# Residual additions ahead of the next evacuation, a row factor made in the feed-forward loop, last output units in halves, first feed-forward tile in two banks

## The chip, the cores and the metric

The kernel runs on one core of a Trainium2 chip. That core has a matrix engine (TensorE, PE in the profile), three engines for elementwise work (VectorE or DVE, ScalarE or ACT, GpSimd or POOL) and a queue engine (SP) that starts most transfers. Each engine runs its own list of instructions in order, and they meet at semaphores. The metric is the device time of one execution in microseconds (us), less is better. Before the change three runs gave 1392.92, 1395.47 and 1396.48 us; the median is 1395.47.

## The reference, cut to what matters

Two blocks of two layers each work on 256 tokens of width 1024, all in float32. The first block has a differential attention layer and a latent attention layer, each followed by a gated feed-forward with a convolution of width 3 and by an embedding that is gated by the residual stream:

```
for i in range(DEPTH):                       # DEPTH = 2
    hn = rms_norm(h, attn_norm[i])
    ...                                      # diff_attention or mla_attention gives mix
    h = h + mix
    h = h + conv_gated_ffn(rms_norm(h, ffn_norm[i]), ffn_w_in[i], ffn_conv_w[i], ffn_conv_b[i], ffn_w_out[i])
    h = h + per_layer_embedding(h, p[i], ple_norm[i], ple_w_proj[i], ple_w_gate[i])

def per_layer_embedding(h, p_i, norm_g, w_proj, w_gate):
    gate = jax.nn.sigmoid(rms_norm(h, norm_g) @ w_gate)
    return (p_i @ w_proj) * gate
```

The second block has a stream x of 256 tokens and a context of 256 tokens. Vectors computed from a conditioning input scale, shift and gate them:

```
mod_x = (silu_c @ w_mod[i] + b_mod[i])[:, None, :]
...
sh_x, sc_x, g_x = jnp.split(mod_x, 3, axis=-1)
hx = rms_norm_2(x, norm_g[i]) * (1.0 + sc_x) + sh_x
hc = rms_norm_2(ctx, norm_g[i]) * (1.0 + sc_c) + sh_c
...                                          # layer 0: grouped attention, layer 1: neighbourhood attention
x = x + g_x * yx
if not last:
    ctx = ctx + g_c * yc
```

## The kernel before, in words

Everything is kept feature-major: `H` holds the residual stream as 8 chunks of 128 features by 256 tokens, `CX` the context. Each product of float32 numbers is made of three matrix products with operands split in a high and a low part (`mm3`, lines 410 to 412). The high part of the activations is in `XH`, the low one in `XL`; of the weights in `WH` and `WL`.

**Weights.** SP reads 295 panels of 128x1024 into six raw slots, in a fixed order (`STREAM`). ScalarE copies a panel to `WH` (line 1729, 1.06 us), VectorE subtracts to `WL` (line 1079, 1.2 us or more). There are only three such pairs of slots (`SPL`), so a panel is split when the third one before it has been used by TensorE. Both engines issue these splits at written places between their other work: a call `ahead(p)` issues all that are due up to panel p+2. What an engine does between two such calls delays the panel that comes next.

**Outputs.** Most products run in units: 128x512 of output in one of two banks, `G0` and `G1` in turn; a unit of a plain product is 2 columns of tiles, 8 input chunks and 3 matmuls, so 48 matmuls of 256 columns, on two panels. A wide unit is 24 matmuls of 512 columns (256 of x and 256 of the context) on one panel. VectorE or ScalarE evacuates a unit and frees its bank. Four more banks are called `A`, and `R` and `O` are two more.

**Norms.** The sum of squares over features is a product with a matrix of ones (`row_stats`, line 464; `col_stats`, line 482, when the result is wanted per token). Squares are made on GpSimd (`squares`, 4 instructions of 128x512, or `sum_of_squares`, which also adds them up, 7 instructions, so that one part instead of four goes through TensorE). ScalarE takes the root (line 1739), VectorE the reciprocal (line 1094). In the first block this factor is applied to the outputs, so products may start before it is there. In the second block it is applied to the inputs: `modulated` has VectorE write x times scale times factor to `XT` (line 1494), ScalarE add the shift and write `XH` (line 2028), and VectorE write `XL` (line 1499), chunk by chunk.

**The places that the change touches**, in the order in which they run, for both layers of the first block where not said otherwise:

- `ffn`: the input projection has 22 tiles of two columns. Tile 0 (`hidden(0, ...)`) needs chunks 6 and 7 of the input last, because they come from the last unit of the attention's output product. All 24 matmuls of its first column come before the 24 of the second. Then come `row_stats`, tile 1, and a loop of tiles with the output projection, which adds up in the four `A` banks.
- `ple`: the small projection `pp` (4 units of 12 matmuls in `G0` and `G1`), then 16 matmuls that turn gathered modulator rows to columns (`turn_gathered`, line 566), then the gate product `pg` (4 units of 48 matmuls). For each unit u of `pg`, VectorE evacuates with the factor (line 1114), ScalarE applies the sigmoid (line 2015), GpSimd multiplies with the projection (line 2354), VectorE adds to `H` (line 1480). In layer 0 the inputs of the next layer (`x_high` and `x_rest` of attn1) are made in between; in layer 1 the context's input for the second block (factor `ac` and `modulated(0, 1, CX, ...)`).
- `l1_dq`: the first product of latent attention, 8 chunks of 6 matmuls of 512 columns; then `col_stats("l1", ...)` with four parts.
- `context_ahead` (layer 1 of the first block is over): 6 chunks of the context go through the query weights while the stream's factor `a` is made; then `row_stats("a")` with four parts, and `wide_unit(0, ...)`, which needs the stream's inputs.
- `a_o`: 8 wide units give the output of the second block's attention; then `row_stats("b")` and the units of `b_q`, whose inputs need `H` after all eight.

## Time and profile before

| what | value |
|---|---|
| median of three runs | 1395.47 us |
| profiled execution, device time | 1392.69 us |
| its span, first to last instruction | 1391.0 us |
| mean granted TensorE clock | 0.979 |
| PE busy | 1297.7 us (93%), 8860 matmuls |
| DVE busy | 948.9 us (68%) |
| ACT busy | 716.7 us (52%) |
| POOL busy | 402.4 us (29%) |
| HBM read | 189.41 MB, 137 GB/s |

The span and the time of the same execution differ by 1.7 us, which lie before the first and behind the last instruction. Busy shares are of the span. A matmul in the trace is shown with its full latency, and the next begins before it ends, so the pace of a row of matmuls is read from their starts, or from a count in a stretch. A row of the timeline reads: start, length, engine, line, operation, output<-inputs, shapes, count; in brackets the idle time of the engine ahead of it and what ended that.

### The profile page before, as it was taken

How to read it: one execution, taken by the hardware profiler on the slowest of the kernel's cores; microseconds unless marked ns; L12 is line 12 of the kernel's file. 1: busy time of each engine (PE TensorE's matmuls, PEld its weight loads, DVE VectorE, ACT ScalarE, POOL GpSimd, SP SyncE). 2: the span in 40 equal slices, each digit the busy share in tenths (PEclk: the TensorE clock that was granted, in tenths of full speed). 3: DMA queues.
4: the chain of work that ended last, by engine and by line, in shares of the span. 5: the costliest groups of instructions: out<-in, count | busy, mean ns of one | idle time of the engine just before them, and what ended most of it. 6: DMA issues, size and time to landing. Idle time of an engine off the chain costs nothing.

```text
span 1391.0 us, 24271 instructions
## 1 busy us (share of the span) xinstructions
PE 1297.7 (93%) x8860; PEld 1122.2 (81%) x8860; DVE 948.9 (68%) x1427; ACT 716.7 (52%) x1244; POOL 402.4 (29%) x390
## 2 busy tenths in 40 slices
PE   6999989999997999998999999699989997999996
PEld 5887979999986876897999998588845586987656
DVE  6868677888866896656888886745257546553674
ACT  5555445555665676544565565433357513412662
POOL 4942234445422140143444542203002311000012
PEclk9999999999998999999999999999999998999999
DMA  8574346666633542153666663222300082532100
GB/s 303 174 233 147 108 140 204 229 222 214 213 117 105 171 133 80 67 191 116 218 226 216 223 211 108 90 92 76 105 16 1 22 210 68 188 104 91 46 1 31
DMA packets 52665, 191.72 MB, mean 138 GB/s; under 512 B 6048, under 2 KB 6304, under 8 KB 52320
## 3 DMA queue, kind: packets, MB, share of 16 engines
q1 hardware_dynamic: 43488, 158.59, 34.3%
q0 software_dynamic: 8368, 31.33, 7.1%
q8 instruction: 62, 1.02, 0.3%
q10 hardware_dynamic: 720, 0.57, 0.1%
q14 instruction: 27, 0.22, 0.1%
HBM read 189.41 MB, written 1.05 MB: 137 GB/s over the span
## 4 chain that ended last, share of the span: by engine, by line
PE 74%; DVE 8%; ACT 7%; issue 7%; POOL 2%; DMA 1%; SPq 0%; DVEq 0%; ACTq 0%; POOLq 0%
PE G L410 13%; PE G L412 12%; PE G L411 12%; PE A L410 6%; PE A L411 5%; PE A L412 5%; PE R L631 3%; DVE WL L1079 2%; ACT WH L1729 2%; PE R L557 2%; PE R L537 2%; PE R L410 1%; PE R L412 1%; PE R L411 1%; PE A L963 1%
## 5 line engine op out<-in xcount | busy, mean ns | idle before, releaser
L1079 DVE TENSOR_TENSOR WL<-RAW,WH 128x1024 fp32r<-128x1024 f32 x295 | 395.1, 1345 | 296.0 <-ACT WH L1729 295.4
L1729 ACT ACTIVATE WH<-RAW 128x1024 fp32r<-128x1024 f32 x295 | 310.3, 1057 | 407.3 <-PE G L412 287.9
L410 PE MATMUL G<-XH,WH 128*128 128x256 f32 (+1 forms) x1368 | 414.5, 303 | 25.4 <-DVE WL L1079 9.5
L411 PE MATMUL G<-XL,WH 128*128 128x256 f32 (+1 forms) x1368 | 410.9, 300 | 0.0
L412 PE MATMUL G<-XH,WL 128*128 128x256 f32 (+1 forms) x1368 | 410.5, 300 | 0.0
L410 PEld LDWEIGHTS G<-XH,WH 128*128 128x128 f32 x1368 | 265.7, 194 | 39.8 <-issue 16.6
L411 PEld LDWEIGHTS G<-XL,WH 128*128 128x128 f32 x1368 | 266.1, 194 | 8.4
L412 PEld LDWEIGHTS G<-XH,WL 128*128 128x128 f32 x1368 | 266.0, 194 | 7.3
L410 PE MATMUL A<-HH,WH 128*128 128x256 f32 x352 | 99.7, 283 | 0.9 <-POOL HL L2333 0.9
L411 PE MATMUL A<-HL,WH 128*128 128x256 f32 x352 | 99.6, 283 | 0.0
L412 PE MATMUL A<-HH,WL 128*128 128x256 f32 x352 | 99.5, 283 | 0.0
L2309 POOL CAST XH<-HRS 128x256 fp32r<-128x256 f32 x24 | 11.4, 474 | 282.7 <-DVE HRS L1653 282.7
L1160 DVE TENSOR_REDUCE SM<-A 128x2 f32<-128x1024 f32 (+1 forms) x80 | 67.9, 850 | 15.2 <-PE A L963 13.5
L410 PE MATMUL G<-WH,XH 128*128 128x512 f32 x136 | 56.4, 415 | 17.3 <-DVE XL L1105 11.2
L410 PEld LDWEIGHTS A<-HH,WH 128*128 128x128 f32 x352 | 67.5, 192 | 2.2 <-ACT WH L1729 1.9
L410 PE MATMUL A<-WH,XH 128*128 128x512 f32 (+1 forms) x144 | 58.1, 403 | 11.5 <-DVE XL L1499 6.1
L411 PEld LDWEIGHTS A<-HL,WH 128*128 128x128 f32 x352 | 67.5, 192 | 0.1
L412 PEld LDWEIGHTS A<-HH,WL 128*128 128x128 f32 x352 | 67.6, 192 | 0.0
L1768 ACT ACTIVATE ATT<-R 128x1024 f32<-128x1024 f32 (+3 forms) x56 | 37.7, 673 | 57.1 <-PE R L631 57.1
L2329 POOL TENSOR_TENSOR HRS<-ATT,HRS 128x256 f32<-128x256 f32 x22 | 31.8, 1444 | 120.1 <-ACT HRS L1934 120.1
L2329 POOL TENSOR_TENSOR HRS<-HSQ,HRS 128x256 f32<-128x256 f32 x22 | 31.8, 1444 | 102.2 <-ACT HRS L1934 102.2
L411 PE MATMUL A<-WL,XH 128*128 128x512 f32 (+1 forms) x144 | 56.4, 391 | 0.0
(346 smaller groups left out, 2474.7 us busy)
## 6 DMA issues: line engine op xcount, KB each, us to landing
RAW<-in_wst SPq DMA_DIRECT2D x295, 512.0 KB, 3.8
M<-in_wmod POOLq DMA_DIRECT2D x48, 512.0 KB, 4.1
B<-in_rpb POOLq DMA_DIRECT2D x4, 1024.0 KB, 11.9
H<-in_x_t SPq DMA_DIRECT2D x2, 512.0 KB, 8.4
M<-in_x_tok SPq DMA_DIRECT2D x1, 1024.0 KB, 13.3
M<-in_ctx_t POOLq DMA_DIRECT2D x1, 1024.0 KB, 6.6
out_y<-M SPq DMA_DIRECT2D x2, 384.0 KB, 2.7
C<-in_cst SPq DMA_DIRECT2D x1, 737.0 KB, 15.4
```

The source lines that it names most:

```text
L410: mm(out, lh, rh, start=start, stop=False, skip_group_check=True)
L411: mm(out, lh, rl, start=False, stop=False, skip_group_check=True)
L412: return mm(out, ll, rh, start=False, stop=stop, skip_group_check=True)
L537: m = mm(out[32 * g:32 * g + 32, q * P:(q + 1) * P], SC[:, k, :], RM[:, i % RMS, k * P:(k + 1) * P], start=(k == 0), stop=(k == KD - 1), s ...
L557: m = mm(O[0:32, :], SCR[:, 2 * s + c, :], w[:, 512 * c:512 * c + 512], start=(s == 0 and c == 0 and w is RH), stop=(s == 3 and c == 1 and ...
L631: m = nc.tensor.transpose(ST[c][:, k * P:(k + 1) * P], PRB[a % 3][:, c, k * P:(k + 1) * P], IDT)
L963: m = mm(out[c][:, 0:nk * P], Q2[64 * c:64 * c + 64, t, qt * P:(qt + 1) * P], K2[64 * c:64 * c + 64, t // 4, k0:512], start=True, stop=Tru ...
L1079: v.tensor_tensor(WL[:, slot, :], RAW[:, raw, :], WH[:, slot, :].bitcast(F32), ALU.subtract).then_inc(w_lo, 1)
L1160: v.tensor_reduce(small(80, a, 2), sc, AX, ALU.max, negate=True).then_inc(at_mx, 1)
L1729: act(WH[:, slot, :], RAW[:, raw, :], ACT.Copy).then_inc(w_hi, 1)
L1768: act(att(s, j)[:, 0:width, 0:nk, q * P:(q + 1) * P], RO[:, :].rearrange("p (l k q) -> p l k q", l=2, k=4)[:, 0:width, 0:nk, :], ACT.Copy) ...
L2329: g.tensor_tensor(HID[b], CB[b][:, 0, :], SG[b], ALU.mult).then_inc(f_hid, 1)
```

## The change

- `ffn`, tile 0: its second column goes to bank `A[3]`; chunks 0 to 5 of both columns come first, then 6 and 7 of both. VectorE evacuates it in two instructions.
- `ple`: units 2 and 3 of `pp` go to `A[0]` and `A[1]`. The 16 turning matmuls become transposes of 32 rows, and VectorE adds the pieces with one reduction. In the loop over the units of `pg`, the addition of unit u-1 and the inputs made from it stand ahead of the evacuation of unit u, on VectorE and on ScalarE.
- The factor `ac` and the first of the three steps of `modulated` for the context move from `ple(1)` into `ffn(1)`; the other two steps stay in `ple(1)`.
- The sums of squares `l1` and `a` are added up on GpSimd, so one part goes through TensorE for each. `row_stats("a")` stands after five chunks of `context_ahead` instead of after all six.
- `a_o`: units 5, 6 and 7 are made in halves: first x of all three (24 matmuls of 256 columns each, banks `A[1]` to `A[3]`), then the context of all three. The sums for `b` and the first inputs for `b_q` go in between.

The core of the diff (the helper functions that split `modulated` in two are the old code cut in two):

```diff
-                hidden(0, p0, u0 % 2, u0 // 2, p0, XS[tag])
+                pe.wait_ge(bank_free[u0 % 2], u0 // 2)
+                for ks in (range(6), range(6, KD)):
+                    for c in range(2):
+                        take(p0 + c)
+                        for k in ks:
+                            x_come(XS[tag], k, KD)
+                            wh, wl = wtile((p0 + c) % SPL, k)
+                            m = mm3((A[3] if c else G[u0 % 2])[:, 0:T], wh, wl, XH[:, k, :], XL[:, k, :], k == 0, k == KD - 1)
+                        if k == KD - 1:
+                            m.then_inc(w_used, 1)
...
                 for u in range(4):
-                    gemm_unit(U0[a] + u, START[a] + u // 2, 4 * (u % 2), 2, 8, 2)
+                    if u >= 2:
+                        pe.wait_ge(h_upd, 8 * layer + u - 1)
+                    gemm_unit(U0[a] + u, START[a] + u // 2, 4 * (u % 2), 2, 8, 2, out=A[u - 2] if u >= 2 else None)
...
-                    m = mm(O[:, 2 * t:2 * t + 2], YR[0:4, 512 + t * P:512 + (t + 1) * P], SEL, start=True, stop=True,
-                           skip_group_check=True)
+                    m = nc.tensor.transpose(O[:, 32 * t:32 * t + 32], YR[:, 512 + t * P:512 + (t + 1) * P], IDT[0:32, 0:32])
...
+                def added(u):
+
+                    dv.wait_ge(p_m, 4 * layer + u + 1)
+                    v.tensor_tensor(flat2(H, u), flat2(H, u), PG[:, u % 2, :], ALU.add).then_inc(h_upd, 1)
+
+                for u in range(4):
+                    e = START[b] + 2 * u + 2
+                    ahead(e - 1)
+                    if u == 0:
+                        row_factor(b, 0)
+                    else:
+                        added(u - 1)
+                        if layer == 0:
+                            x_rest(H, "attn1", 0, 2 * u, 2 * u - 2)
+                        elif u < 3:
+                            modulated_rest(0, 1, range(4 * u - 4, 4 * u))
+                    if u >= 2:
+                        dv.wait_ge(h_upd, 8 * layer + 4 + u - 1)
+                    evac(U0[b] + u, e, PG[:, u % 2, :].rearrange("p (a t) -> p a t", a=2), 0)
+                    ahead(e)
+                added(3)
...
+            for u in range(5, 8):
+                part_o(u, A[u - 4][:, 0:T], 0).then_inc(ao_x, 1)
+                if u == 6:
+                    row_stats("b", R, range(0, 2))
+            for u in range(5, 8):
+                part_o(u, bank(U0["a_o"] + u)[:, T:512], 8).then_inc(w_used, 1)
+                if u == 5:
+                    row_stats("b", R, range(2, 4))
...
-            squares("l1", H, updated(4))
+            sum_of_squares("l1", H, updated(4))
...
-            squares("a", H, updated(12))
+            sum_of_squares("a", H, updated(12))
```

VectorE in `ple(0)`, from the factor to the evacuation of the last unit of `pg`. `ATP<-G,RST` is an evacuation, `H<-H,ATP` an addition, `XL<-H,V,XH` an input of the next layer. Before:

```order
L1094 RECIPROCAL RST<-RST 128x256 [waits row_rt]
L1114 TENSOR_TENSOR ATP<-G,RST 128x512 [waits w_used,row_ok]
L1079 TENSOR_TENSOR WL<-RAW,WH 128x1024 [waits w_hi] x2
L1114 TENSOR_TENSOR ATP<-G,RST 128x512 [waits w_used]
L1480 TENSOR_TENSOR H<-H,ATP 128x512 [waits p_m]
L1079 TENSOR_TENSOR WL<-RAW,WH 128x1024 [waits w_hi] x2
L1114 TENSOR_TENSOR ATP<-G,RST 128x512 [waits w_used,h_upd]
L1480 TENSOR_TENSOR H<-H,ATP 128x512 [waits p_m]
L1079 TENSOR_TENSOR WL<-RAW,WH 128x1024 [waits w_hi]
L1105 SCALAR_TENSOR_TENSOR XL<-H,V,XH 128x256 [waits x_hi] x2
L1079 TENSOR_TENSOR WL<-RAW,WH 128x1024 [waits w_hi]
L1114 TENSOR_TENSOR ATP<-G,RST 128x512 [waits w_used,h_upd]
```

The same stretch of VectorE now, where the names are the same and the lines are those of the changed kernel:

```order
L1121 RECIPROCAL RST<-RST 128x256 [waits row_rt]
L1141 TENSOR_TENSOR ATP<-G,RST 128x512 [waits w_used,row_ok]
L1106 TENSOR_TENSOR WL<-RAW,WH 128x1024 [waits w_hi] x2
L1527 TENSOR_TENSOR H<-H,ATP 128x512 [waits p_m]
L1132 SCALAR_TENSOR_TENSOR XL<-H,V,XH 128x256 [waits x_hi] x2
L1141 TENSOR_TENSOR ATP<-G,RST 128x512 [waits w_used]
L1106 TENSOR_TENSOR WL<-RAW,WH 128x1024 [waits w_hi] x2
L1527 TENSOR_TENSOR H<-H,ATP 128x512 [waits p_m]
L1132 SCALAR_TENSOR_TENSOR XL<-H,V,XH 128x256 [waits x_hi] x2
L1141 TENSOR_TENSOR ATP<-G,RST 128x512 [waits w_used,h_upd]
```

Each addition and its two input instructions moved from behind the next evacuation to ahead of it.

VectorE at the end of `a_o` and the start of `b_q`. `H<-G,MD,H` adds the x part of a unit, `M<-G,MD,M` its context part (`CX` lies in `M`); `M<-H,GS,RST` and `XL<-M,MD,XH` make the inputs. Before, from the x part of the last unit:

```order
L1661 SCALAR_TENSOR_TENSOR H<-G,MD,H 128x256 [waits w_used]
L1663 SCALAR_TENSOR_TENSOR M<-G,MD,M 128x256
L1094 RECIPROCAL RST<-RST 128x256 [waits row_rt]
L1494 SCALAR_TENSOR_TENSOR M<-H,GS,RST 128x256 [waits row_ok]
L1494 SCALAR_TENSOR_TENSOR M<-H,GS,RST 128x256 x7
L1499 SCALAR_TENSOR_TENSOR XL<-M,MD,XH 128x256 [waits x_hi] x8
```

The same place now, from the x parts of the last three units:

```order
L1702 SCALAR_TENSOR_TENSOR H<-A,MD,H 128x256 [waits ao_x] x3
L1707 SCALAR_TENSOR_TENSOR M<-G,MD,M 128x256 [waits w_used]
L1106 TENSOR_TENSOR WL<-RAW,WH 128x1024 [waits w_hi]
L1121 RECIPROCAL RST<-RST 128x256 [waits row_rt]
L1434 SCALAR_TENSOR_TENSOR M<-H,GS,RST 128x256 [waits row_ok]
L1434 SCALAR_TENSOR_TENSOR M<-H,GS,RST 128x256 x3
L1707 SCALAR_TENSOR_TENSOR M<-G,MD,M 128x256 [waits w_used]
L1442 SCALAR_TENSOR_TENSOR XL<-M,MD,XH 128x256 [waits x_hi] x4
L1106 TENSOR_TENSOR WL<-RAW,WH 128x1024 [waits w_hi]
L1434 SCALAR_TENSOR_TENSOR M<-H,GS,RST 128x256 x4
L1442 SCALAR_TENSOR_TENSOR XL<-M,MD,XH 128x256 [waits x_hi] x4
```

The context parts and two weight splits now stand among the steps that make the inputs of `b_q`, and these come four chunks at a time.

## Rows read from the trace of the kernel before

**Rows 1.** Page, part 4, the chain that ended last by engine

```profile
PE 74%; DVE 8%; ACT 7%; issue 7%; POOL 2%; DMA 1%; SPq 0%; DVEq 0%; ACTq 0%; POOLq 0%
```

**Rows 2.** Waits of PE: engine line <- releaser: total us, times, longest

```profile
PE G L410 <- DVE XL L1105: 17.6, 5, 11.2
PE G L410 <- DVE WL L1079: 9.5, 7, 2.2
```

**Rows 3.** Windows, PE alone: stretch, its length, busy (x matmuls), clock, DMA share, GB/s

```profile
1112.00:1132.00 20.00, 20.00 (x90) 1.00 1.01 241
1182.00:1202.00 20.00, 20.00 (x169) 1.00 0.59 198
1156.00:1166.00 10.00, 4.51 (x21) 0.50 0.01 2
...
852.00:856.00 4.00, 4.00 (x23) 0.57 0.40 137
```

**Rows 4.** Timeline, PE, tile 0 of the feed-forward in layers 0 and 1

```profile
177.10 0.36 PE L410 MATMUL G<-XH,WH 128*128 128x256 f32 x1 [2.19 <-DVE XL L1105]
...
181.81 1.02 PE L464 MATMUL R<-RSQ,C 128*128 128x256 f32 x4
...
628.91 0.35 PE L410 MATMUL G<-XH,WH 128*128 128x256 f32 x1 [2.60 <-DVE XL L1105]
...
635.12 1.02 PE L464 MATMUL R<-RSQ,C 128*128 128x256 f32 x4
```

**Rows 5.** Timeline, PE, ple of layer 0 and the start of l1_dq

```profile
391.71 0.39 PE L410 MATMUL G<-XH,WH 128*128 128x256 f32 x1 [0.93 <-ACT B L1986]
...
394.78 3.77 PE L566 MATMUL R<-C,B 4*128 4x2 f32 x32
...
406.43 0.47 PE L410 MATMUL G<-XH,WH 128*128 128x256 f32 x1
...
425.71 0.47 PE L410 MATMUL G<-WH,XH 128*128 128x512 f32 x1 [0.90 <-issue]
```

**Rows 6.** Timeline, ACT, after the evacuation of unit 1 of pg

```profile
414.69 0.63 ACT L2015 ACTIVATE ATP<-ATP 128x512 f32<-128x512 f32 x1 [2.32 <-DVE ATP L1114]
415.23 2.10 ACT L1729 ACTIVATE WH<-RAW 128x1024 fp32r<-128x1024 f32 x2
```

**Rows 7.** Timeline, DVE, the same unit and the last of layer 1

```profile
416.30 2.61 DVE L1079 TENSOR_TENSOR WL<-RAW,WH 128x1024 fp32r<-128x1024 f32 x2 [1.05 <-ACT WH L1729]
...
419.76 0.68 DVE L1480 TENSOR_TENSOR H<-H,ATP 128x512 f32<-128x512 f32 x1
...
422.89 0.87 DVE L1105 SCALAR_TENSOR_TENSOR XL<-H,V,XH 128x256 fp32r<-128x256 f32 x2
...
885.23 0.68 DVE L1114 TENSOR_TENSOR ATP<-G,RST 128x512 f32<-128x512 f32 x1
```

**Rows 8.** Timeline, PE, chunk 6 of l1_dq, col_stats and the next product

```profile
438.13 0.47 PE L410 MATMUL G<-WH,XH 128*128 128x512 f32 x1 [2.39 <-issue]
...
442.39 1.99 PE L482 MATMUL R<-C,RSQ 128*128 128x2 f32 x16
...
449.85 0.61 PE L410 MATMUL A<-WH,XH 128*128 128x320 f32 x1 [2.70 <-ACT WH L1729]
```

**Rows 9.** Groups by line, POOL: busy us, mean ns of one, idle before

```profile
L2251 POOL TENSOR_TENSOR RSQ<-H 128x512 f32<-128x512 f32 x10 | 13.9, 1404 | 20.8 <-PE R L482 12.8 <-DVE H L1712 8.1
...
L2269 POOL TENSOR_TENSOR RSQ<-RSQ 128x512 f32<-128x512 f32 x4 | 6.9, 1730 | 0.3
```

**Rows 10.** Timeline, PE, from the context's product to wide_unit

```profile
877.39 0.35 PE L410 MATMUL G<-XH,WH 128*128 128x256 f32 x1 [2.14 <-DVE WL L1079]
...
893.72 1.89 PE L464 MATMUL R<-HSQ,C 128*128 128x256 f32 x8
...
901.74 0.77 PE L410 MATMUL A<-WH,XH 128*128 128x512 f32 x1 [6.13 <-DVE XL L1499]
```

**Rows 11.** Timeline, PE, from the sums for b to the end of unit 0 of b_q

```profile
1152.87 1.13 PE L464 MATMUL R<-ATP,C 128*128 128x256 f32 x4 [1.39 <-POOL ATP L2251]
...
1161.49 0.55 PE L410 MATMUL G<-XH,WH 128*128 128x256 f32 x1 [7.49 <-DVE XL L1499]
...
1169.44 1.89 PE L464 MATMUL R<-HSQ,C 128*128 128x256 f32 x8
```

**Rows 12.** Groups by line, DVE

```profile
L1094 DVE RECIPROCAL RST<-RST 128x256 f32<-128x256 f32 x9 | 15.8, 1750 | 14.6 <-ACT RST L1739 14.6
...
L1494 DVE SCALAR_TENSOR_TENSOR M<-H,GS,RST 128x256 f32<-128x256 f32 x16 | 7.9, 561 | 0.1
```

More of the change, by code:

```diff
@@ L429, in x_come, with gemm_unit @@
                     pe.wait_ge(x_lo, fresh - per * (kt - 1 - k))
-            def gemm_unit(u, p, first, kt, x, ncol, width=T, xh=XH, xl=XL, fresh=None, per=1):
-                out = bank(u)
+            def gemm_unit(u, p, first, kt, x, ncol, width=T, xh=XH, xl=XL, fresh=None, per=1, out=None):
+                if out is None:
+                    out = bank(u)
                 i = first
@@ L854, in _ @@
                     token_unit(u, 0, 512, 2, XS["l1"] - KD)
-                    col_stats("l1", R, [RSQ[:, i % 2, :] for i in range(4)])
+                    col_stats("l1", R, [RSQ[:, 0, :]])
                 elif name == "ckv":
@@ L1452, in ffn @@
                     turn(j % 2, (u0 + j) % 2, j, p, p + 3, p + 3, hb + j)
+                    if layer == 1 and j == 2:
+                        row_factor("ac", 1)
+                    elif layer == 1 and j < 5:
+                        modulated_full(0, 1, CX, range(4 * j - 12, 4 * j - 8))
                 with dv.Fori(0, GROUPS) as i:
@@ L1919, in ffn @@
                 root(tag, 0, D)
+                if layer == 1:
+                    root("ac", 1, D, R[:, T:2 * T])
                 ahead(p0 + 2)
@@ L2184, in _ @@
             attention("a")
-            for u in range(8):
+            for u in range(6):
                 ahead(START["a_o"] + u + 1)
             root("b", 0, D)
-            modulated(1, 0, 16, range(KD))
+            modulated(1, 0, 16, range(4))
+            ahead(START["a_o"] + 7)
+            modulated(1, 0, 16, range(4, KD))
             for u in range(4):
```

127 lines of the change are left out of this document (68 added, 59 removed).

## The prediction, made before the changed kernel was run

> **What bounds the kernel now.** I first read the chain that ended last. TensorE holds 74% of it, VectorE and ScalarE 8% and 7%, transfers 1% [rows 1]. So a change pays where it removes matmul time or a hole between matmuls, and a faster transfer pays nothing. Next I read TensorE's waits. The largest sums are for the low part of the inputs and for the low part of the weights [rows 2]. 11.2 us of the first lie at the very start, which the change leaves alone. The timeline of TensorE at the places that the change names then shows holes of 2.19 and 2.60 us in tile 0 of the feed-forward [rows 4], 0.93 us in pp [rows 5], 2.70 us behind the sums of l1 [rows 8], 2.14 and 6.13 us ahead of the second block [rows 10], and 1.39 and 7.49 us between a_o and b_q [rows 11].
>
> I read two paces of matmul from the windows. 90 of 512 columns in 20 us make 0.222 us each, and 169 of 256 columns in 20 us make 0.118 us each, both at a clock of 1.00 [rows 3], which is the 2.4 GHz level. So halving a matmul's width nearly halves its time. The clock is part of the account too. After the turning matmuls it is 0.57 for 4 us. Around the hole of 7.49 us it is 0.50, the 1.2 GHz level, from 1156 to 1166 [rows 3]. A unit of 48 matmuls that costs 48 x 0.118 = 5.7 us elsewhere took 1169.44 - 1161.49 = 8.0 us there [rows 11]. A filled hole can therefore give back about 1.5 to 2.3 us of slow matmuls besides itself.
>
> The sum is made against the profiled execution, 1392.69 us for a span of 1391.0, so it is in microseconds of that trace. The median of the three runs is 2.8 us higher, and I take the difference off the median.
>
> **Tile 0 of the feed-forward, gain 4.0.** The last two chunks of input arrive as late as before. Of the 24 matmuls of the second column, 18 now run ahead of them, so the sums start 18 x 0.118 = 2.1 us earlier than 181.81 [rows 4]. What follows is a chain through the root, the reciprocal, the evacuation and the next split, and it keeps its length. The evacuation in two pieces adds an estimated 0.2 us to it, since a DVE instruction of half the width costs a little more than half. Layer 0 gives 1.9. In layer 1 the first wait to the sums took 635.12 - 628.91 = 6.2 us, against 181.81 - 177.10 = 4.7 us in layer 0 [rows 4]. The 1.5 us more are the slow clock, and a hole cut from 2.60 to about 0.4 us should spare them. Against that stand the root of ac on ScalarE in front of the next split (about 0.4 us), and a reciprocal of 1.75 us and 8 products of 0.56 us [rows 12] that VectorE now does among tiles 2 to 4. Its idle time per tile there is about as long as each insertion, so only the first, straight behind a wait, should be felt: 0.9 us. Layer 1 gives 2.1 + 1.5 - 0.2 - 0.4 - 0.9 = 2.1. Bounds of the pair: 2 (clock slow anyway, all insertions felt) to 5.7.
>
> **Front of ple, 3.8 us earlier in each layer.** The hole of 0.93 goes, since units 2 and 3 of pp wait for no bank. The 16 turning matmuls are 32 records and took 3.77 us, 0.118 each [rows 5], as long as a matmul of 256 columns. The trace shows no transpose of this shape. From above each takes what the pair takes (gain 0). From below it costs one record (gain 1.9). I take 1.9, since a record of 4x2 already costs the least that TensorE shows here. With 1 us of the slow clock behind them this puts the start of unit 1 of pg at 402.6 instead of 406.43 [rows 5]. At that point the panel behind it limits, not TensorE.
>
> The clock at 852 to 856 is 0.57 right behind matmuls that touch 4 rows and 2 columns [rows 3]. Transposes of 32 rows might keep the clock up or might not. The Trainium skill ("TensorE: Matmul & The Clock Gate", Part 4: PE-mode transpose) says that transposes do not count as activity of TensorE for the clock. That speaks against this part of the change. By it the slow stretch stays and unit 1 starts 1.1 us later in each layer, 2.2 us in all, which would make the forecast 1378. No run here shows it yet.
>
> **The moved additions, a loss of 5.3 inside ple(0).** Evacuation u+1 now stands behind the addition of unit u and behind the inputs made from it. From one evacuation to the next VectorE and ScalarE then need: evacuation 0.68, sigmoid 0.63, two copies of a panel 2.10 [rows 6], the second subtraction 1.3 of the 2.61, addition 0.68 [rows 7], ScalarE's high parts about 0.9, and half of the 0.87 for the low parts [rows 7]. Together that is 6.8 us. TensorE needs 5.7 for a unit. So ple(0) is no longer paced by TensorE but by this ring: the first evacuation at 405.6 (402.6, plus the split of the next panel 1.3 and the reciprocal 1.75 [rows 12]), the fourth at 405.6 + 3 x 6.9 = 426.3 (0.1 for the semaphores), and l1_dq starts at 427.2 instead of 425.71 [rows 5]. The 3.8 us of the front are spent, and 1.5 more.
>
> **l1_dq and its sums, net gain of layer 0 5.5.** The inputs of chunks 0 to 5 are now ready when l1_dq starts. The fourth weight panel still is not. ScalarE copies it behind ten input copies in both kernels, so chunk 6 starts at 437.6, about where it did (438.13 [rows 8]), and the product ends at 440.4. Before it ended at 442.39 [rows 8]. The sums then have a quarter of the matmuls: 1.2 us instead of 449.85 - 2.70 - 442.39 = 4.8 [rows 8]. The wait of 2.70 behind them stays, because ScalarE still issues the next panel only behind the root. The next product starts at 440.4 + 1.2 + 2.7 = 444.3 instead of 449.85 [rows 8]: 5.5 us. What hides the longer work of GpSimd is l1_dq itself. Seven instructions, 4 x 1.40 + 3 x 1.73 = 10.8 us [rows 9], begin behind the fourth evacuation, sigmoid and product, at 429.2, and end at 440.0, 0.4 us before they are wanted. If that cover goes, each us shows. Bounds: 2.5 to 7.
>
> **Layer 1, from pp to the first product with x, gain 3.0.** The front gives 3.8 as in layer 0. The hole of 2.14 [rows 10] came from context work between the evacuations. It shrinks to about 1.5, since the copy for that panel now waits behind the later evacuation of unit 1. The last evacuation stood at 885.23, well behind TensorE [rows 7], and comes at about 879, so GpSimd begins its squares 6.3 us earlier. But it has 10.8 us of work instead of 4 x 1.40 = 5.6 [rows 9], 5.2 us more. TensorE has done five of six chunks by then and waits for the sum. The sums go from eight matmul pairs to two, about 2.8 us less of TensorE, but most of these ran beside the squares, so I count 1.9. The factor is ready 6.3 - 5.2 + 1.9 = 3.0 us earlier, and the hole of 6.13 behind it [rows 10] becomes 4.7 plus the sixth chunk: 901.74 becomes 898.7. Bounds: 0.5 to 5.5.
>
> VectorE works beside those GpSimd instructions, and these additions took 1.73 us in the mean against 1.40 of the squares [rows 9]. The Trainium skill ("SBUF — State Buffer", Who interferes with whom) says that a VectorE instruction with two SBUF inputs and a GpSimd instruction that reads SBUF exclude each other for whole instructions. By it the seven instructions keep these means or go above them, towards the first rival below.
>
> **a_o in halves, gain 7.0.** Three units of 24 wide matmuls become 48 narrow ones each: 3 x (48 x 0.118 - 24 x 0.222) = 1.0 us added. From the last sums at 1152.87 to b_q at 1161.49 lie 8.6 us of root, reciprocal and inputs [rows 11]. Now two context halves, 48 x 0.118 = 5.7 us, run beside them, and only 4 of the 8 first steps stand ahead of chunk 0 (4 x 0.56 = 2.2 us [rows 12]). So chunk 0 waits for nothing, and chunk 4 waits about 2.6 us for the second four and the weight split between them. Holes of 1.39 + 7.49 = 8.9 become 2.9: 6.0 less. The slow clock cost unit 0 of b_q 8.0 - 5.7 = 2.3, of which I count 2.0. Sum: 6.0 + 2.0 - 1.0 = 7.0. Bounds: 4.5 (a new slow stretch) to 8.
>
> **Sum.** 4.0 + 5.5 + 3.0 + 7.0 = 19.5 us. The median goes from 1395.5 to 1376.0.
>
> **Rivals.**
> - *The ring and the sums on GpSimd take ple and what follows back.* If the ring is 8 us instead of 6.8, and GpSimd needs 2 us per instruction, the 5.5 and 3.0 go to zero: 19.5 - 8.5 = 11 us, 1384.5. For it: both have almost no slack (0.4 us in l1_dq). Against it: the long rows of GpSimd stand beside heavy VectorE work, which is thinner after the last evacuation.
> - *The clock gives more.* If the slow stretches in l1_dq, behind the sums of l1 and ahead of the second block all go too, at 1.5 to 2 us each, and tile 0 gives its upper bound, the gain is about 27: 1368.5. Against it: these stretches stand behind holes that remain in part.
> - *Slower.* The moved addition couples the units fully: the copy of unit u+2's first panel waits for the evacuation of unit u+1. Then TensorE (5.7) and the way from an evacuation to a ready panel (0.68 + 0.63 + 1.05 + 1.3 = 3.6) run one after the other in all 8 units: 8 x 3.6 = 29 us on top of the forecast, 1405. It decides once an evacuation ends later than the unit behind it begins its second half. Against it: the first panel of unit u+2 is issued right behind the sigmoid of unit u, with a unit of 5.7 us to spare.
> - *No change.* The waits move to the weight splits everywhere, and the gain stays below 4 us.
>
> **How the numbers follow.** Forecast 0.58, the ring and GpSimd 0.22, more from the clock 0.10, no change 0.05, slower 0.05. The range goes from 1368 to 1387, which takes in the first two rivals and the bounds (gains of 9 to 27). A measurement of this kernel can tell about 0.3%, 4 us, from no change. Faster by more than that: 0.58 + 0.22 + 0.10 = 0.90, taken as 0.89; within it 0.06; slower 0.05.
>
> **What would show it.** Right: between the first wait of tile 0 and its sums about 2.5 us in both layers; no wait in pp; 16 transposes in under 2 us; four evacuations of ple(0) 6.8 us apart; sums of l1 in 1.2 us; unit 0 of b_q with a wait near 2.6 us and a clock of 1.00. Wrong: evacuations at TensorE's pace of 5.8 us (the gain in layer 0 grows), a wait of TensorE for GpSimd ahead of the sums of l1, a clock of 0.5 behind the transposes or in b_q, or new waits of more than 1 us in tiles 3 to 5 of ffn(1).

## The result

| kernel | median | runs | ratio to the kernel before, 95% interval |
|---|---|---|---|
| before | 1395.08 us | 4 (1392.92 to 1396.48) | |
| changed | 1380.97 us | 4 (1380.17 to 1383.41) | 0.9903 (0.9885 to 0.9922) |

The change makes the kernel 14.1 us faster, by the medians. The prediction was 1376.0 with a range of 1368 to 1387. So the sign and the range were right, and the forecast was 5.0 us too low. Two later executions, 3170.83 us of "order undone" and 4345.82 of "GpSimd waits", stand apart from all others and are left out below.

The profiled execution of the changed kernel took 1383.41 us for a span of 1381.7. It was the slowest of its four, while that of before (1392.69) was quicker than the four runs in the table. So the two traces differ by 9.3 us only. TensorE's mean granted clock was 0.976 in it and 0.979 before. (1 - clock) x span is the time that TensorE's clock withheld: 33.2 us against 29.2. So the clock withheld 4.0 us more in this trace than in that of before; without that the two would differ by an estimated 13.3 us, near the 14.1 of the medians.

The chain of the changed kernel by engine, to be held against [rows 1]:

```profile
PE 72%; DVE 10%; ACT 8%; issue 5%; POOL 2%; DMA 1%; SPq 0%; DVEq 0%; ACTq 0%; POOLq 0%
```

VectorE has gained 2 points of it. TensorE's waits in the changed kernel (total, times, longest) show where, against [rows 2]:

```profile
PE R L466 <- POOL RSQ L2340: 7.0, 1, 7.0
...
PE G L411 <- DVE ATP L1141: 4.7, 1, 4.7
PE G L411 <- issue: 4.2, 1, 4.2
```

They are 7.0 us for GpSimd's sum, 4.7 for an evacuation, and 4.2 put down to "issue". The first two are new; the third stood at the same chunk before, with 2.39 us [rows 8]. The next rows, the timeline of TensorE in the changed kernel, say where they lie:

```profile
178.97 1.02 PE L466 MATMUL R<-RSQ,C 128*128 128x256 f32 x4
...
199.26 0.36 PE L411 MATMUL G<-XH,WH 128*128 128x256 f32 x1 [2.37 <-DVE WL L1106]
...
392.27 1.19 PE L568 MATMUL R<-C,B 32*128 32x32 f32 x16
394.50 0.55 PE L411 MATMUL G<-XH,WH 128*128 128x256 f32 x1 [1.04 <-ACT B L2057]
401.77 1.02 PE L466 MATMUL R<-RSQ,C 128*128 128x256 f32 x4
...
426.69 0.76 PE L411 MATMUL G<-WH,XH 128*128 128x512 f32 x1 [4.69 <-DVE ATP L1141]
441.78 0.47 PE L411 MATMUL G<-WH,XH 128*128 128x512 f32 x1 [4.22 <-issue]
446.20 0.95 PE L484 MATMUL R<-C,RSQ 128*128 128x2 f32 x8
449.85 0.60 PE L411 MATMUL A<-WH,XH 128*128 128x320 f32 x1 [2.70 <-ACT WH L1798]
...
632.01 0.36 PE L411 MATMUL G<-XH,WH 128*128 128x256 f32 x1 [0.46 <-DVE XL L1132]
634.57 1.03 PE L466 MATMUL R<-RSQ,C 128*128 128x256 f32 x4
...
854.82 1.02 PE L466 MATMUL R<-RSQ,C 128*128 128x256 f32 x4
890.64 2.05 PE L466 MATMUL R<-RSQ,C 128*128 128x256 f32 x4 [7.01 <-POOL RSQ L2340]
898.82 0.77 PE L411 MATMUL A<-WH,XH 128*128 128x512 f32 x1 [3.57 <-DVE XL L1442]
...
1154.16 0.36 PE L411 MATMUL G<-XH,WH 128*128 128x256 f32 x1 [2.52 <-ACT XH L2096]
1160.17 1.89 PE L466 MATMUL R<-HSQ,C 128*128 128x256 f32 x8
```

- Tile 0: the sums of layer 0 start 2.8 us earlier than in [rows 4], of which 0.7 was there before the tile. The row at 199.26 is the wait of tile 3 for a weight split (an expectation below calls it tile 2's); before it was 0.95 us, at 202.06. In layer 1 from the first wait to the sums it is 634.57 - 632.01 = 2.56 us; it was 6.2.
- Front of ple: 16 transposes take 1.19 us instead of 3.77 [rows 5]. But now the first unit of pg waits 1.04 us for ScalarE's copy out of its bank.
- Product behind l1: 449.85 in both traces [rows 8], to the hundredth. Nothing of the 5.5 us arrived.
- First product with x: 898.82 instead of 901.74 [rows 10].
- End of unit 0 of b_q: 1160.17 instead of 1169.44 [rows 11], which is the whole 9.3 us of the span. Behind it nothing changes.

VectorE and GpSimd in the changed kernel around the start of l1_dq, the place where the account goes wrong:

```profile
412.05 0.68 DVE L1141 TENSOR_TENSOR ATP<-G,RST 128x512 f32<-128x512 f32 x1
...
418.98 0.68 DVE L1141 TENSOR_TENSOR ATP<-G,RST 128x512 f32<-128x512 f32 x1
...
431.71 8.82 DVE L1132 SCALAR_TENSOR_TENSOR XL<-H,V,XH 128x256 fp32r<-128x256 f32 x10 [0.58 <-ACT XH L1816]
440.46 1.21 DVE L1106 TENSOR_TENSOR WL<-RAW,WH 128x1024 fp32r<-128x1024 f32 x1
```

```profile
428.56 3.47 POOL L2337 TENSOR_TENSOR RSQ<-H 128x512 f32<-128x512 f32 x2
432.12 1.35 POOL L2339 TENSOR_TENSOR RSQ<-RSQ 128x512 f32<-128x512 f32 x1
...
437.35 1.32 POOL L2340 TENSOR_TENSOR RSQ<-RSQ 128x512 f32<-128x512 f32 x1
```

Ten input subtractions take 8.82 us, where two took 0.87 [rows 7]. Five of them last 1.25 to 1.52 us each while GpSimd's row goes on; once it has ended, at 438.67, the last four take 0.40 each. Only then, at 440.46, can VectorE write the low part of the fourth weight panel, for which chunk 6 waits. "issue" in TensorE's wait hides that, because the last semaphore of several is not always the one the profile names.

In the kernel before, twelve such subtractions took 4.83 us at this place, because GpSimd stood still beside them. It waited for the sums to free its two buffers:

```profile
443.57 2.04 POOL L2251 TENSOR_TENSOR RSQ<-H 128x512 f32<-128x512 f32 x2 [12.78 <-PE R L482]
```

The sum on GpSimd needs no further buffer, so that pause is gone, and with it VectorE's free stretch.

The clock, from windows of TensorE alone in the changed kernel (length, busy, clock, DMA share, GB/s):

```profile
200.00:210.00 10.00, 10.00 (x73) 0.84 0.90 308
...
394.00:396.00 2.00, 1.50 (x7) 0.59 0.31 45
...
425.00:430.00 5.00, 3.31 (x8) 0.51 0.46 154
430.00:435.00 5.00, 5.00 (x20) 0.81 0.32 105
...
450.00:460.00 10.00, 10.00 (x53) 0.71 0.66 198
...
540.00:550.00 10.00, 8.21 (x34) 0.66 0.17 52
...
1150.00:1160.00 10.00, 7.47 (x47) 0.83 0.32 107
1154.16:1160.17 6.01, 6.01 (x37) 0.72 0.40 140
```

Before, the windows at 450, 540 and 1150 had 0.85, 0.83 and 0.80, and that at 200 had 1.00. The hole of 4.69 us is followed by a clock of 0.51, where there was 1.00, but TensorE waited for chunk 6 afterwards, so that one cost nothing. From 450 to 550 two stretches are slower than before although the kernels do the same there. So from 449.85, where both traces stood, this one comes to the first wait of the next tile 0 at 632.01, 3.1 us behind [rows 4]. That stretch took 182.2 us here, 179.1 before, and 178.8 to 182.3 in the other kernels, which do the same work there.

### The profile page after: what moved, and what is told of

The parts are those of the page before. It is cut to its first block, busy times and chain, and to the rows that moved or that the text cites. A ratio compares the mean times of both kernels' runs of the same rounds, so it can differ in the third digit from the quotient of the medians.

```text
span 1381.7 us, 24316 instructions
## 1 busy us (share of the span) xinstructions
PE 1290.4 (93%) x8864; PEld 1117.4 (81%) x8864; DVE 954.6 (69%) x1431; ACT 716.7 (52%) x1244; POOL 412.0 (30%) x396
## 4 chain that ended last, share of the span: by engine, by line
PE 72%; DVE 10%; ACT 8%; issue 5%; POOL 2%; DMA 1%; SPq 0%; DVEq 0%; ACTq 0%; POOLq 0%
PE G L411 12%; PE G L413 12%; PE G L412 12%; PE A L411 5%; PE A L413 5%; PE A L412 5%; DVE WL L1106 4%; PE R L632 3%; ACT WH L1798 2%; PE R L559 2%; PE R L539 2%; PE R L411 1%; PE R L413 1%; PE R L412 1%; PE A L974 1%
## 5 line engine op out<-in xcount | busy, mean ns | idle before, releaser
L411 PE MATMUL G<-XH,WH 128*128 128x256 f32 (+1 forms) x1336 | 401.3, 300 | 18.5 <-DVE WL L1106 11.6
L412 PE MATMUL G<-XL,WH 128*128 128x256 f32 (+1 forms) x1336 | 397.7, 298 | 0.0
L413 PE MATMUL G<-XH,WL 128*128 128x256 f32 (+1 forms) x1336 | 397.4, 297 | 0.0
L411 PEld LDWEIGHTS G<-XH,WH 128*128 128x128 f32 x1336 | 258.0, 193 | 32.3 <-issue 12.2
L412 PEld LDWEIGHTS G<-XL,WH 128*128 128x128 f32 x1336 | 258.2, 193 | 7.5
L413 PEld LDWEIGHTS G<-XH,WL 128*128 128x128 f32 x1336 | 258.3, 193 | 6.3
L1187 DVE TENSOR_REDUCE SM<-A 128x2 f32<-128x1024 f32 (+1 forms) x80 | 67.9, 850 | 15.1 <-PE A L974 13.4
L411 PE MATMUL G<-WH,XH 128*128 128x512 f32 x136 | 57.5, 423 | 20.8 <-DVE XL L1132 10.2
L413 PE MATMUL A<-WH,XL 128*128 128x512 f32 (+1 forms) x144 | 57.2, 397 | 0.0
```

The source lines that it names most:

```text
L411: mm(out, lh, rh, start=start, stop=False, skip_group_check=True)
L412: mm(out, lh, rl, start=False, stop=False, skip_group_check=True)
L413: return mm(out, ll, rh, start=False, stop=stop, skip_group_check=True)
L1187: v.tensor_reduce(small(80, a, 2), sc, AX, ALU.max, negate=True).then_inc(at_mx, 1)
```

## The experiments

Unless said otherwise a kernel is the changed one with one part edited, and differences are to its 1380.97 us. The kernels ran in several groups, each beside the kernel before, whose median there lay between 1392.80 and 1395.08. So the ratios compare more fairly than the medians, and the third column turns them into us against the changed kernel (1394 us for a ratio of 1). The half width of a ratio's interval is about 0.0018, 2.5 us, so a difference between two of them is known to some 3.5 us. Places in a trace are sharper, and I read those first.

| kernel | median | by the ratio, against changed | ratio to before, interval | clock |
|---|---|---|---|---|
| changed | 1380.97 | | 0.9903 (0.9885 to 0.9922) | 0.976 |
| sums early | 1380.76 | +0.1 | 0.9904 (0.9887 to 0.9921) | 0.979 |
| four parts | 1375.07 | -4.7 | 0.9869 (0.9852 to 0.9887) | 0.983 |
| halves undone | 1386.04 | +7.2 | 0.9955 (0.9939 to 0.9971) | 0.979 |
| order undone | 1378.57 | -2.2 | 0.9887 (0.9871 to 0.9903) | 0.979 |
| four parts, order undone | 1371.76 | -8.9 | 0.9839 (0.9821 to 0.9856) | 0.982 |
| front undone | 1387.67 | +6.6 | 0.9950 (0.9937 to 0.9963) | 0.977 |
| tile 0 undone | 1385.27 | +4.5 | 0.9935 (0.9918 to 0.9952) | 0.979 |
| factor back | 1386.23 | +6.3 | 0.9948 (0.9931 to 0.9966) | 0.981 |
| squares on ScalarE | 1366.07 | -13.4 | 0.9807 (0.9787 to 0.9827) | 0.985 |
| GpSimd waits | 1381.70 | +1.7 | 0.9915 (0.9891 to 0.9939) | 0.976 |

### GpSimd waits for VectorE

```diff
+            gp.wait_ge(x_lo, XS["l1"])
             sum_of_squares("l1", H, updated(4))
```

> The changed kernel, but GpSimd starts its sum of squares for l1 only once VectorE has made all inputs of l1_dq, so that the two never work side by side there. Theory A (they shut each other out, instruction by instruction): each input subtraction takes 0.40 to 0.43 us instead of 1.35, chunk 6 starts near 437.6 instead of 441.78; each of GpSimd's seven takes 1.10 to 1.36 us, 8.6 in all from 436.5, so the sums start near 445.2 instead of 446.20 and the next product near 449 instead of 449.85. Theory B (the subtractions are slow for a reason of their own, as a transfer or the clock): they keep 1.35 us, chunk 6 stays near 441.8, the sums start near 448.5 and the next product near 452.

VectorE, then GpSimd, then TensorE in this kernel, where l1_dq starts at 428.12, 1.43 us later than in the changed kernel's trace (1.39 of it from before tile 0):

```profile
432.31 4.08 DVE L1132 SCALAR_TENSOR_TENSOR XL<-H,V,XH 128x256 fp32r<-128x256 f32 x10 [0.58 <-ACT XH L1816]
...
436.47 3.02 POOL L2337 TENSOR_TENSOR RSQ<-H 128x512 f32<-128x512 f32 x2 [6.42 <-DVE XL L1132]
...
445.82 1.87 PE L484 MATMUL R<-C,RSQ 128*128 128x2 f32 x8 [3.97 <-POOL RSQ L2340]
450.39 0.61 PE L411 MATMUL A<-WH,XH 128*128 128x320 f32 x1 [2.70 <-ACT WH L1798]
```

Ten subtractions take 4.08 us, 0.41 each, and the wait ahead of chunk 6 is gone: it comes 10.9 us behind the start of l1_dq instead of 15.1. The last twelve wide matmuls take 2.7 us, at full clock, where they took 4.4 behind the hole. Theory A is shown at this place: side by side the two engines shut each other out. From the start of l1_dq to the next product it is 22.3 us against 23.2, the 0.9 us that A gave; the wait has only moved to the sums, 3.97 us for GpSimd. The whole kernel is no faster. So neither place for the seven instructions is free: beside VectorE they delay the inputs, behind it the sum.

The Trainium skill ("SBUF — State Buffer", Who interferes with whom) says that VectorE instructions with two SBUF inputs and GpSimd instructions that read SBUF contend for a shared port, and that the lock holds for a whole instruction. The traces agree: a subtraction that takes 0.41 us alone takes 1.25 to 1.52 beside GpSimd, about as long as the one instruction of GpSimd (1.10 to 1.37 us) that runs meanwhile.

### Four parts instead of one sum

```diff
-        SUMMED = {..., "l1": RSQ, "ac": ATP, ..., "a": RSQ}
+        SUMMED = {..., "ac": ATP, ...}
+        SQX["l1"] = SQX["a"] = [RSQ[:, 0, :], RSQ[:, 1, :], HSQ[:, 0, :], HSQ[:, 1, :]]
-            sum_of_squares("l1", H, updated(4))
+            squares("l1", H, updated(4))
...
-            sum_of_squares("a", H, updated(12))
+            squares("a", H, updated(12))
```

> The changed kernel, but l1 and a are not added up on GpSimd: it makes only the four squares of each, into four buffers of their own, and TensorE adds them (16 small matmuls for l1, 8 for a). Theory A (VectorE is shut out while GpSimd works, and in layer 1 TensorE waits for GpSimd): four instructions instead of seven shut VectorE out, so chunk 6 of l1_dq starts near 439 instead of 441.78, the sums take 2 us instead of 1, the next product starts near 448 instead of 449.85; in layer 1 the squares end near 886.2 instead of 890.5, and the first product with x comes near 895.5 instead of 898.8. Together 4 to 6 us faster than the changed kernel, 1375 to 1377. Theory B (GpSimd is not what delays chunk 6): chunk 6 stays at 441.8, the sums cost 1 us more, layer 1 still gains 3: 1378 to 1380.

```profile
432.04 5.74 DVE L1133 SCALAR_TENSOR_TENSOR XL<-H,V,XH 128x256 fp32r<-128x256 f32 x10 [0.58 <-ACT XH L1817]
...
439.01 0.47 PE L412 MATMUL G<-WH,XH 128*128 128x512 f32 x1 [0.85 <-issue]
448.16 0.60 PE L412 MATMUL A<-WH,XH 128*128 128x320 f32 x1 [2.70 <-ACT WH L1799]
...
852.72 1.02 PE L467 MATMUL R<-RSQ,C 128*128 128x256 f32 x4
...
891.09 0.77 PE L412 MATMUL A<-WH,XH 128*128 128x512 f32 x1 [4.74 <-DVE XL L1443]
```

Theory A gave 439 and 448 in layer 0, and both came. In layer 1 it gave 895.5, and the product came at 891.09. In layer 1, from the sums of pg to the first product with x it is 38.4 us against 898.82 - 854.82 = 44.0. The median is 5.9 us lower, by the ratios 4.7. The summing on GpSimd, a part of the change, costs more than it saves. For l1 the kernel before had two buffers, and the second half of its squares waited for them. With four buffers the same 32 small matmuls take 448.16 - 2.70 - 441.84 = 3.6 us instead of 4.8 [rows 8], so the third and fourth buffer bring 1.1 us. Its sum for a had four buffers already.

### Sums early

```diff
                     g.tensor_tensor(PG[:, u % 2, :], PG[:, u % 2, :], flat2(PJ, u), ALU.mult).then_inc(p_m, 1)
+                    if u:
+                        sum_early(("l1", "a")[layer], H, updated(4 + 8 * layer), u - 1)
+                sum_early(("l1", "a")[layer], H, updated(4 + 8 * layer), 3)
```

> The changed kernel, but GpSimd does the steps of the sums of squares l1 and a for the pairs 0, 1 and 2 inside the loop over the units of pg, each right behind its product with the projection; only the last square and the last addition (1.1 + 1.3 us) remain behind the loop. Theory A: in the changed kernel GpSimd's row of seven instructions shuts VectorE out of its input subtractions at the start of l1_dq (nine of them took 8.43 us), and in layer 1 the row is itself what TensorE waits for. By it chunk 6 of l1_dq starts near 437.5 instead of 441.78, the next product at 444 to 446 instead of 449.85, and the first product with x near 892 instead of 898.8; since GpSimd then takes part of VectorE's time inside the loop, the evacuations stand 7 to 8 us apart instead of 6.92, which costs 0 to 3 us per layer. In all 5 to 12 us faster than the changed kernel: 1369 to 1376. Theory B: what delays chunk 6 is the later end of ple(0) and the slow clock behind the hole of 4.69 us, not GpSimd. Then the next product stays at 449 to 451, only layer 1 gains, and the whole comes to 1375 to 1380. Theory C: any GpSimd work in the loop stretches the ring by its whole length, 2.4 us per unit, and the kernel is no faster: 1380 to 1388.

VectorE in ple(0) of this kernel, a pair of weight splits and the two evacuations behind them (the one ahead stood at 412.45):

```profile
414.78 3.46 DVE L1106 TENSOR_TENSOR WL<-RAW,WH 128x1024 fp32r<-128x1024 f32 x2 [1.65 <-ACT WH L1798]
...
420.22 0.68 DVE L1141 TENSOR_TENSOR ATP<-G,RST 128x512 f32<-128x512 f32 x1
...
429.09 0.68 DVE L1141 TENSOR_TENSOR ATP<-G,RST 128x512 f32<-128x512 f32 x1
```

I had leaned to A; the total is C's. The two splits take 3.46 us instead of 2.61 [rows 7], the ring grows from 6.9 to 7.8 and 8.9 us, less than the 2.4 per unit of C, and l1_dq starts 3.2 us later. In layer 1 the first product with x comes 43.3 us behind the sums of pg, so 0.7 is gained there. In all nothing. GpSimd's squares run beside the weight splits here, and the splits stand in the ring; VectorE's idle time lies elsewhere in the unit.

### Order undone, and both together

```diff
-                    if u == 0: row_factor(b, 0)
-                    else: added(u - 1); x_rest(H, "attn1", 0, 2 * u, 2 * u - 2)
...
                     evac(U0[b] + u, e, PG[:, u % 2, :].rearrange("p (a t) -> p a t", a=2), 0)
+                    if u:
+                        added(u - 1)
                     ahead(e)
+                    if layer == 0 and u >= 2:
+                        x_rest(H, "attn1", 0, 2 * u - 2, 2 * u - 4)
```

(The same on ScalarE, and `modulated_rest` in layer 1.)

> The changed kernel, but in ple the addition of unit u-1 and the inputs made from it stand again behind the evacuation of unit u, on VectorE and on ScalarE, in both layers. Theory A (the moved additions tie the evacuations into a ring of 6.92 us, against 5.7 of TensorE for a unit): evacuations in ple(0) 5.8 us apart, l1_dq starts near 422.5 instead of 426.69; the input subtractions behind it still run against GpSimd's seven instructions, so chunk 6 starts near 439 to 440 instead of 441.78 and the next product near 447 instead of 449.85; layer 1, where VectorE and GpSimd set the end, 0 to 1 us earlier. 3 to 4 us faster than the changed kernel: 1377 to 1378. Theory B (the moved additions feed the inputs of the next layer early and so pay for themselves): what the loop gains comes back as a later chunk 6, and the kernel is 0 to 4 us slower than the changed one: 1381 to 1385.

> The changed kernel with four parts for l1 and a (GpSimd makes the squares alone, into four buffers) and, besides, the old order of additions and evacuations in ple. Against the kernel with four parts alone (1375.07, next product behind the sums of l1 at 448.16). Theory A (ring and GpSimd are two costs that add up): chunk 6 of l1_dq near 436, next product near 445.5, 2.7 us less: 1372. Theory B (VectorE's total work up to chunk 6 decides, in whatever order it stands): chunk 6 stays at 438.5 to 439.5, next product 447.5 to 448.5, no change: 1374 to 1376.

TensorE with the order undone, the sum on GpSimd kept:

```profile
422.05 0.47 PE L411 MATMUL G<-WH,XH 128*128 128x512 f32 x1 [0.90 <-issue]
...
438.75 0.77 PE L411 MATMUL G<-WH,XH 128*128 128x512 f32 x1 [5.24 <-issue]
...
447.30 0.61 PE L411 MATMUL A<-WH,XH 128*128 128x320 f32 x1 [2.70 <-ACT WH L1800]
```

The same two places with four parts as well:

```profile
433.66 0.49 PE L412 MATMUL G<-WH,XH 128*128 128x512 f32 x1 [3.26 <-issue]
...
445.11 0.61 PE L412 MATMUL A<-WH,XH 128*128 128x320 f32 x1 [2.70 <-ACT WH L1801]
```

l1_dq starts at 422.05 instead of 426.69. Of these 4.6 us 1.6 are lost again up to chunk 6, since more subtractions now stand against GpSimd, and 0.5 behind it. In layer 1, from the sums of pg to the first product with x, it is 42.2 us instead of 44.0, 1.8 less where A had at most 1. In the median it is 2.4 us less (2.2 by the ratios), short of the 3 to 4 of theory A and within what can't be told from nothing; the places in the trace side with A. With four parts as well it is 1371.76, 3.3 us below four parts alone (4.2 by the ratios), where A had 2.7; the two places came at 433.66 and 445.11, where A had 436 and 445.5. So ring and GpSimd are two costs that add up, and the moved additions, the first item of the title, are a loss of 2 to 4 us.

### The parts that pay, undone one by one

Halves:

```diff
-            for u in gemm_wide("a_o", 5, None, 1):
+            for u in gemm_wide("a_o", 8, None, 1):
```

> The changed kernel with a_o as before: all its units wide, the sums for b and all inputs of b_q behind them. Theory A (the halves are the largest gain): holes of 1.4 and 7.5 us come back ahead of b_q, with slow matmuls behind them, and 1.0 us of narrow matmuls goes: 6.0 us slower than the changed kernel, 1387 (bounds 4.5 to 8). Theory B (a good part of the gain at this place was the clock of one execution): 2 to 4 us slower, 1383 to 1385.

Front of ple:

```diff
-                    gemm_unit(..., out=A[u - 2] if u >= 2 else None)
+                    gemm_unit(...)
...
-                    m = nc.tensor.transpose(O[:, 32 * t:32 * t + 32], YR[:, ...], IDT[0:32, 0:32])
+                    m = mm(O[:, 2 * t:2 * t + 2], YR[0:4, ...], SEL, start=True, stop=True, skip_group_check=True)
```

> The changed kernel, but all four units of pp go to the two banks G0 and G1 again, and the gathered rows are turned by the 32 small matmuls. Theory A (the front of ple gives what the timeline shows, 4.0 and 3.9 us, and all of it reaches the end): 7.9 us slower than the changed kernel, 1389. Theory B (behind the front the evacuations and GpSimd decide, so part of a later front is hidden): 3 to 5 us slower, 1384 to 1386. In both the 32 matmuls take 3.8 us against 1.2 of the 16 transposes, and a slow stretch of TensorE's clock stands behind them in both layers.

Tile 0:

```diff
-                for ks in (range(6), range(6, KD)): ...
+                hidden(0, p0, u0 % 2, u0 // 2, p0, XS[tag])
```

> The changed kernel, but tile 0 of the feed-forward is made in one bank again, its first column ahead of its second. Theory A (tile 0 gives the 4.0 us of the prediction): 4 us slower than the changed kernel, 1385. Theory B (in layer 0 the 2.1 us come back as longer waits of the next tiles for a weight split, as the hole of 2.37 us in tile 2 suggests, and only layer 1 gains): 1 to 2.5 us slower, 1382 to 1383.5. In both the first wait of tile 0 to its sums takes 4.7 us and more instead of 2 to 2.6.

Context factor:

```diff
                         elif u < 3:
-                            modulated_rest(0, 1, range(4 * u - 4, 4 * u))
+                            if u == 1:
+                                row_factor("ac", 1)
+                            modulated(0, 1, CX, range(4 * u - 4, 4 * u))
```

> The changed kernel, but the context's factor ac and the first of its three steps are made in ple(1) again, between the evacuations. Theory A (VectorE's 1.75 + 8 x 0.41 = 5.0 us there lie on the way to the last evacuation, while in the feed-forward they are hidden): the last evacuation comes 4 to 5 us later than 878.10, the first product with x near 903 instead of 898.8, of which 0.4 to 1.3 us is given back in tile 1 and 2 of ffn(1): 3 to 4 us slower than the changed kernel, 1384 to 1385. Theory B (GpSimd's sum of squares decides the end of ple(1), and VectorE's insertions fit beside it or cost as much in the feed-forward): within 1 us of the changed kernel, 1380 to 1382.

TensorE ahead of b_q with the halves undone, and between two units of pg with the factor back:

```profile
1155.06 0.55 PE L411 MATMUL G<-XH,WH 128*128 128x256 f32 x1 [7.49 <-DVE XL L1436]
```

```profile
868.92 0.55 PE L411 MATMUL G<-XH,WH 128*128 128x256 f32 x1 [4.40 <-DVE WL L1106]
```

- Halves: the hole of 7.49 us is back, and the kernel is 5.1 us slower by the medians (7.2 by the ratios), on either side of theory A's 6.0.
- Front: 6.7 us slower, nearer to A (7.9) than to B. Read from the start of pp to the sums of pg, it is 18.0 us in both layers with the old front. With the new one it is 15.35 in layer 0 and 13.9 in layer 1, a gain of 2.7 + 4.1 = 6.8.
- Tile 0: 4.3 us slower by the medians, the total of theory A. The sums start 3.6 us later in layer 0 and, measured from the small product at 513, 2.2 in layer 1. But 1.5 of the 3.6 are a slow stretch of the clock in tile 0 (0.70 from 177 to 181) that the kernel before did not have there [rows 4]; it took 4.7 us from the first wait to the sums and this one 6.2.
- Factor: 5.3 us slower (6.3 by the ratios), above A. The insertions make one evacuation late, TensorE gets a hole of 4.40 us (1.06 in the changed kernel), and from the sums of pg to the first product with x it is 48.9 us instead of 44.0. In the feed-forward the same work costs 0.4 us.

By the medians the parts sum to 5.1 + 6.7 + 4.3 + 5.3 - 2.4 for the order - 5.9 for the sums on GpSimd = 13.1 us, against 14.1 measured. By the ratios they sum to 17.7, against 13.5. Each carries some 3 us of uncertainty, so neither sum tests the split. Not undone by itself was the new place of `row_stats("a")`, and the banks of pp and the transposes were only undone together.

### A better version: squares on ScalarE

Four parts, the old order in ple, and ScalarE makes the squares for l1 and a:

```diff
+            def squares_here(name, ready):
+                ac.wait_ge(row_mm, RSW[name][0])
+                for i in range(4):
+                    ready(2 * i)
+                    act(SQX[name][i], flat2(H, i), ACT.Square).then_inc(row_sq, 1)
...
                     ahead(START["l1_dq"] + 1)
+                    squares_here("l1", updated(4))
...
+            squares_here("a", updated(12))
             root("a", 0, D)
```

> The kernel with four parts and the old order in ple (1371.76), but ScalarE makes the squares for l1 and a, four instructions of about 0.61 us each, and GpSimd none. Theory A (what GpSimd still takes from VectorE at these places is time on the path): the twelve input subtractions ahead of chunk 6 take 0.40 us each, so chunk 6 of l1_dq starts 1 to 2 us earlier; in layer 1 the last square is ready 1.5 to 2 us earlier. 2 to 4 us less: 1368 to 1370. Theory B (with four squares alone GpSimd is already off the path, and ScalarE's squares stand in front of its weight splits): no change or slower, 1371 to 1374.

VectorE, ScalarE and TensorE, with l1_dq starting at 422.93:

```profile
427.79 4.83 DVE L1133 SCALAR_TENSOR_TENSOR XL<-H,V,XH 128x256 fp32r<-128x256 f32 x12
...
432.87 1.13 ACT L1828 ACTIVATE RSQ<-H 128x512 f32<-128x512 f32 x2
...
434.32 0.47 PE L412 MATMUL G<-WH,XH 128*128 128x512 f32 x1 [1.62 <-issue]
...
443.69 0.61 PE L412 MATMUL A<-WH,XH 128*128 128x320 f32 x1 [2.70 <-ACT WH L1801]
```

Twelve subtractions take 4.83 us, and from the start of l1_dq to the next product it is 20.8 us; it was 25.0 with GpSimd's squares. Of these 4.3 us 2.2 come up to chunk 6. Another 1.6 are the last twelve wide matmuls, 2.8 us at full clock behind a hole of 1.62 against 4.4 behind one of 3.26, and 0.5 are the sums. From the transposes of ple on the gain is 3.2, since l1_dq itself started 1.1 us later here, behind a slow stretch of the clock. In layer 1 it gains nothing: 36.6 us from the sums of pg to the product with x in both. The median is 1366.07, 5.7 us less than without it (4.5 by the ratios, known to 3.7), more than theory A's 2 to 4. The clock goes with the surplus: it is 0.985 against 0.982, which withholds 20.5 us instead of 24.7. This kernel is faster than the kernel before and than the changed one: its ratio to before, 0.9807, has an interval that stays below all of the changed kernel's.

## Why the prediction was right, and where it was not

- **Tile 0, 4.0**: undoing it costs 4.3 to 4.5, and between the traces it is 0.6 + 3.2 = 3.8. The total is right, the split is luck. In layer 0 the 2.1 us arrive at tile 3 (199.26 against 202.06, with 0.7 from before), but behind its hole of 2.37 a slow stretch (0.84 from 200 to 210) takes 1.5 of them back before pp; 1.9 had been forecast, 0.6 came. In layer 1 it is 3.2 from the first wait to pp, where 2.1 had been forecast.
- **Front, 3.8 in each layer**: 2.7 and 4.1. The transposes were cheaper than I took (1.19, not 1.9), but a wait of 1.04 for ScalarE's copy behind them was not in the forecast. The slow stretch that I let go is still there in layer 0 (0.59 from 394) and gone in layer 1. The Trainium skill ("TensorE: Matmul & The Clock Gate", Part 4: PE-mode transpose) says that transposes don't count as activity; by it the forecast would have lost 1.1 us in each layer. Layer 0 agrees with that, layer 1 does not. In the ten kernels with transposes the 2.5 us of pg behind them have a clock of 0.50 to 0.61 in layer 0 six times and in layer 1 twice, and 1.00 the other twelve times; in the two kernels with the 32 small matmuls it is 0.50 to 0.57 all four times. So the transposes spared the slow stretch more often than not, and what decides in a single case stays open.
- **Ring, a loss of 5.3 in ple(0)**: evacuations 412.05 and 418.98 are 6.93 us apart (forecast 6.8 to 6.9). l1_dq starts at 426.69 (forecast 427.2), but pp had started 1.3 us early, so it is 0.8 late by the sum, which is what the front fell short of. The mechanism and its size are right.
- **l1_dq and its sums, net gain of layer 0 5.5**: this is the step that failed. The prediction had chunk 6 at 437.6 and the next product at 444.3. They came at 441.78 and 449.85. Since pp had started 1.3 us earlier (386.42 against 387.74), layer 0 lost 1.3 where a gain of 5.5 was forecast, 6.8 us off. 0.8 of them was there when l1_dq started. 4.7 arise up to chunk 6, 15.1 us where 10.4 had been forecast: that is VectorE shut out by GpSimd's seven instructions, which the prediction had called hidden by l1_dq itself, and 4.2 us go away when GpSimd waits. Another 1.6 is a term that was too small: the last twelve wide matmuls took 446.20 - 441.78 = 4.4 us, behind a hole, where 12 x 0.222 = 2.7 was counted. The kernel before had shown it: there the same twelve took 442.39 - 438.13 = 4.3 us [rows 8], both numbers of the prediction. The sums gave 0.25 back. I had weighed only whether GpSimd would be ready in time (it was, at 438.67). I never asked whom it would hold up meanwhile, though the rule that I cited for layer 1 says it for both engines. The first rival had the right suspects, but by the ring's length, which held, and by a GpSimd of 2 us per instruction, where the seven took 10.1 in all.
- **Layer 1 to the first product with x, 3.0**: 898.82 against a forecast of 898.7, with pp starting within 0.1 us of the trace before. The terms hold too: the last evacuation at 878.10 (forecast 879), GpSimd's longer row behind it, and TensorE waiting for the sum, 7.01 us. What undoing adds is their size: the factor in the feed-forward brings about 5, and the sum on GpSimd takes more than 5 back.
- **a_o in halves, 7.0**: 6.0 in the traces, from the hole of 8.9 that became 2.52 at chunk 4 (forecast 2.6). Of the 2.0 us that the clock was to give back little came: behind that hole it was 0.72 for 36 matmuls, which took 6.0 us instead of 36 x 0.118 = 4.2, where I had forecast 1.00.

Along the two traces the 9.3 us are 0.7 before tile 0, 0.6 for tile 0, -1.3 for ple(0) and l1_dq, -3.1 of clock up to the next tile 0, 3.2 for it, 2.8 up to the product with x, 0.4 on the way to a_o and 6.0 there. The forecast had 19.5. The result lies in the range because the range was wide enough for a rival that took back layer 0's gain; the single forecast missed it. Of the signs of being wrong that it named one showed, in both its places: a slow clock behind the transposes (layer 0) and in unit 0 of b_q.

## What to carry to other kernels

Ask of work given to an idle engine not only when it ends but whom it shuts out: here a VectorE subtraction took as long as the GpSimd instruction beside it, and in layer 0 ScalarE did the same squares at no such price. Before a wait for a buffer is removed, ask who works undisturbed during it. And price every part by undoing it: this change was four parts of 4 to 7 us that pay and two that take back 7 to 8.
